# Second-table rows of the expert stage requested at the step that uses them, not three steps earlier

## The reference

```
e = top experts of the token, (512 tokens, 8 heads, 16)      # indices into both tables
a = gelu(einsum('nhkd,nd->nhk', u_tab[e], x))                # first table: 128 rows of 1024 floats per token
out = einsum('nhk,nhkd->nd', softmax(score) * a, v_tab[e])   # second table: 128 rows of 1024 floats per token
```

## Time and profile before

| | us |
|---|---|
| median of 3 runs | 3035.53 |
| lowest and highest run | 3022.3, 3048.35 |
| the profiled execution, its own time | 3030.12 |
| its span from first to last instruction | 3028.4 |
| first dot product of the expert stage starts at | 878.9 |
| last dot product, last addition of a v row start at | 2795.4, 2847.7 |

### The profile page before, as it was taken

How to read it: one execution, slowest core, us unless ns; L and a number is a source line. 1 busy time by engine, 2 the same in 40 slices (tenths; PEclk the granted TensorE clock), 3 DMA queues, 4 the chain that set the end, 5 groups by cost and what they waited for, 6 DMA issues and landing times. The chain is left out here.

```text
span 3028.4 us, 26320 instructions
## 1 busy us (share of the span) xinstructions
PE 1817.3 (60%) x7725; PEld 1085.1 (36%) x7725; DVE 1847.8 (61%) x4141; ACT 392.8 (13%) x991; POOL 1312.7 (43%) x1187
## 2 busy tenths in 40 slices
PE   3999789699805569445652565675212420685585
PEld 2356466454402124222211444572112320565311
DVE  3145367731177966678997667678546884786313
ACT  1010146420101000011100111110000100110000
POOL 1000000000036754557877545565477776775202
PEclk7999879899957879767985787658655555555597
DMA  2222220034248999999999999788578996999673
GB/s 55 90 79 89 86 84 2 1 112 152 104 147 291 346 401 353 328 358 330 341 353 364 375 354 359 292 330 302 170 264 276 338 349 234 355 327 373 235 266 112
DMA packets 279873, 740.18 MB, mean 244 GB/s; under 512 B 47921, under 2 KB 91466, under 8 KB 279154
## 3 DMA queue, kind: packets, MB, share of 16 engines
q0 software_dynamic: 156672, 564.61, 51.2%
q1 hardware_dynamic: 121890, 169.67, 16.1%
q10 hardware_dynamic: 1168, 4.23, 0.4%
HBM read 729.91 MB, written 12.56 MB: 245 GB/s over the span
## 5 line engine op out<-in xcount | busy, mean ns | idle before, releaser
L3050 POOL DMA_INDIRECT branch_rows_t<-in_v_tab,e_idx x437 | 513.1, 1174 | 328.9 <-DVE heads_t L3086 190.4
L3041 POOL DMA_INDIRECT ex_u<-in_u_tab,e_idx x257 | 287.1, 1117 | 534.8 <-POOLq L2944 431.6
L3086 DVE SCALAR_TENSOR_TENSOR heads_t<-branch_rows_t,ex_coef,heads_t 128x1024 f32<-128x1024 f32 x339 | 434.5, 1282 | 4.1 <-DMA branch_rows_t<-in_v_tab,e_idx 1.4
L3070 DVE CUSTOM_DVE_ANT_0 ex_u<-ex_u,heads_t 128x1024 f32<-128x1024 f32 x257 | 314.0, 1223 | 178.7 <-DMA ex_u<-in_u_tab,e_idx 172.5
L3070 DVE CUSTOM_DVE_ANT_0 heads_t<-heads_t 128x1024 f32<-128x1024 f32 x255 | 311.5, 1222 | 176.4 <-DMA heads_t<-in_u_tab,e_idx 167.3
L3041 POOL DMA_INDIRECT heads_t<-in_u_tab,e_idx x255 | 286.2, 1122 | 98.7 <-issue 75.5
L3143 PE MATMUL ex_y_ps<-branch_rows_t,heads_t 128*128 128x512 f32 x392 | 206.8, 664 | 117.5 <-ACT heads_t L3113 48.0
L1281 PE MATMUL cs_pp<-cs_ch,xn_t 128*128 128x256 f32 x512 | 143.4, 449 | 173.9 <-DMA cs_ch<-in_cache_cmp_kv 173.9
L788 PE MATMUL in_acc<-in_w,xn_t 128*128 128x512 f32 (+7 forms) x560 | 203.0, 519 | 8.7 <-DMA in_w<-in_w_in 8.2
L1281 PEld LDWEIGHTS cs_pp<-cs_ch,xn_t 128*128 128x128 f32 x512 | 116.2, 230 | 203.3 <-DMA cs_ch<-in_cache_cmp_kv 123.4
L3143 PEld LDWEIGHTS ex_y_ps<-branch_rows_t,heads_t 128*128 128x128 f32 x392 | 76.0, 209 | 241.5 <-issue 144.3
(11 more groups left out here) (718 smaller groups left out, 3197.4 us busy)
## 6 DMA issues: line engine op xcount, KB each, us to landing
cs_ch<-in_cache_cmp_kv SPq DMA_DIRECT2D x256, 128.0 KB, 7.3
fq_mg_wg<-in_w_gate SPq DMA_DIRECT2D x6, 2048.0 KB, 20.3
fs_mg_wg<-in_w_gate SPq DMA_DIRECT2D x6, 2048.0 KB, 9.6
in_w<-in_w_in SPq DMA_DIRECT2D x4, 2048.0 KB, 7.8
branch_rows_t<-in_v_tab,e_idx POOLq DMA_INDIRECT x437, 6.3
first_w<-in_w_gate SPq DMA_DIRECT2D x3, 2048.0 KB, 7.8
fp_wb<-in_w_branch SPq DMA_DIRECT2D x6, 1024.0 KB, 10.1
fp_wg<-in_w_gate SPq DMA_DIRECT2D x3, 2048.0 KB, 7.9
```

What stands on the lines that cost most here:

```text
L3041: pool.indirect_dma_start(out=u(s), out_offset=None, in_=i["u_tab"], in_offset=bass.IndirectOffsetOnAxis(ap=idx[:, t, m:m + 1], axis=0)).t ...
L3050: pool.indirect_dma_start(out=v(n), out_offset=None, in_=i["v_tab"], in_offset=bass.IndirectOffsetOnAxis(ap=idx[:, t, m:m + 1], axis=0)).t ...
L3070: dve.tensor_tensor_reduce(out=u(s), in0=u(s), in1=x(t), scale=1.0, scalar=0.0, op0=ALU.mult, op1=ALU.add, accum_out=dots[:, t, m:m + 1]). ...
L3086: dve.scalar_tensor_tensor(out=y(t), in0=v(n), scalar=coef[:, t, m:m + 1], in1=y(t), op0=ALU.mult, op1=ALU.add).then_inc(acc_done, 1)
```

## The change

GpSimd issues v(s - 24) at step s in place of v(s - 21), at the very step at which VectorE or TensorE uses it. The diagonals of ScalarE keep their 21.

```
@@ mix_prompt, the gpsimd program
-                    n = s - LAG + AHEAD
+                    n = s - LAG
                     if 0 <= n < NS:
                         t, m = at(n)
                         if n == V_MOVES:
                             pool.wait_ge(beside.ended, merged)
                         if n >= NV_BUF:
                             mixed(pool, n - NV_BUF)
                         pool.indirect_dma_start(out=v(n), ...)
```

## The result

The changed kernel takes 3049.3 us (median of 14 executions, 3040.61 to 3055.65), the kernel before 3035.32 us (14 executions, 3022.3 to 3048.35) on the same chip: ratio 1.0045, 95% interval 1.0029 to 1.0061. The forecast was 3027 us, 0.3% less; it is 0.45% more. The profiled execution has a span of 3048.3 us, against 3028.4.

What follows compares the result with a forecast made beforehand. Gather DMA, VectorE and GpSimd were taken to stand within 15% of one another, so it was read window by window. The terms, -9 - 3 - 2 + 4 + 1 = -9 us, took the 3035.5 us median to 3027 us; range 2996 to 3068 us.

Steps and rivals of the forecast that it cites:

- part 1: 1050 to 1400 and 1650 to 1900 us, GpSimd with slack: u's lead brings half of 17.5 unfilled us, -9 us.
- part 2: Windows with GpSimd full: lead can't be used; -3 us for late windows, between 0 and -15; side gathers' stretches 0.
- contention: Slower rival: TensorE's 16 waits for the compression's loads grow by two gathers each, +46 us, 3080 us; chance 0.04.
- Part 1's second window: 1650 to 1900 us: DMA share 1.01, nothing unfilled; VectorE waits longer for TensorE (55.6 us), so nothing counted.
- Part 3: At 2149 us: GpSimd's 12.87 us wait for TensorE before a v row goes, but only two u rows come earlier, -2 us.
- Part 4: v without a reserve: additions wait for v in part of the steps; bounds nothing and 45 us, taken +4 us.
- Part 5: The ends: start unaffected; at the tail 24 v rows left after the last u row, not 21; +1 us.
- the faster rival: Same as "The lead is worth its waits": 2962 us at its end, 2990 us if half comes; chance 0.15.
- v just in time: Slower rival: additions wait 0.4 us in each of the full windows' 113 steps, nothing gives it back, 3075 us; chance 0.08.
- The lead is worth its waits: Faster rival: all 66 us of u waits in two windows and 12 of the late ones go, 2962 us; chance 0.15.

Runs made afterwards that it cites:

- e9: Against the kernel before (v 21 slots behind): 24 behind in steps 0 to 199 and from 460 on; 3085.14 us, ratio 0.9962.
- e11: Against the kernel before (v 21 slots behind): 24 behind only from step 460 on; 3084.68 us, ratio 0.9957.
- e12: Against the kernel before (v 21 slots behind): 24 behind in steps 224 to 343 and from 460 on; 3030.93 us, ratio 0.9989.
- e14: Against the kernel before (v 21 slots behind): 24 behind only from step 460 on, same as e11 on another chip; 3022.08 us, ratio 0.9961.
- e1: Against the kernel before (v 21 slots behind): 24 behind only in steps 200 to 223, the compression's weights; 3045.96 us, ratio 1.0029.
- e2: Against the changed kernel (v 24 slots behind): 21 behind in steps 200 to 223; 3046.02 us, ratio to the kernel before 1.0040.
- e4: Against the changed kernel (v 24 slots behind): 21 behind in steps 200 to 223 and 344 to 459; 3028.91 us, ratio to the kernel before 0.9984.
- e7: Against the kernel before (v 21 slots behind): 24 behind only in steps 344 to 459, the side gathers' stretches; 3123.11 us, ratio 1.0035.
- e8: Not the layer: GpSimd issues five times 24 gathers, beside VectorE idle, dot products, additions, and both with pauses, compared with one another; 240.26 us.

## Why the prediction was wrong

The sum ended at -9 us; the changed kernel is 14 us slower. Three steps failed: that half of the unfilled DMA share could be had (part 1), that the side gathers' stretches keep their length because the count for a step is the same (part 2), and that contention costs nothing because "what the loads lose the gathers have already got". The time still lies inside 2996 to 3068 us, and that is luck: losses of 26 us and a gain of 12 us, none of them in the sum at near its size, cancel in part. The terms, by their own numbers:

- *Part 1, -9 us: measured 0.* The wait for u did go, nearly all of it (49.1 to 3.8 us in the first window). The step that failed is the one from the DMA share: that half of the 17.5 unfilled us could be had. Where the waits for u went, the waits for the side lane took over 44 of the 45 us. e9 equals e11, and steps 0 to 210 are 701.6 to 711.1 us with 21 behind and 702.1 to 711.7 with 24.
- *Part 1's second window, counted within it as nothing: measured +9 us* (e12 less e14), and up to +9 us for the weights just ahead of it (e1: 0.0029 of 3032). I had put the contention rival at "what the loads lose the gathers have already got". For the six loads of the weights it matters when GpSimd pauses (4.6 against 20.8 us, and 4.7 with the wait put back). For the compression the times say that the old pause is worth 9 us; VectorE's wait for TensorE there grew by 24 us (55.6 to 79.7), and through which load, no run tells.
- *Part 2, -3 us, "the lead can't be used": wrong on both sides.* The side gathers' stretches, put at 0, cost 13 us in the steps of the changed kernel and 17 in the times of e2 and e4 (7 to 11 by e7 on its chip). At the end, where I had GpSimd at 94%, the lead was worth 12 us (e14 0.9961 of 3034), the one gain of the change. The fullness was read from busy time at the durations of before. A busy time that holds 1.04 us issues isn't a fixed length: 0.94 us when VectorE is idle, up to 3.01 us when not.
- *Part 3, -2 us.* The wait of 12.87 us went, and as the text had it the same stage waited for VectorE instead. The timeline after, answering to the earlier trace rows, shows the new wait in full (14.91 us where 12.87 and 0.64 had been, so nothing came back):

```profile
2166.61 0.94 POOL L3050 DMA_INDIRECT branch_rows_t<-in_v_tab,e_idx  x1 [0.30 <-issue]
2182.46 1.91 POOL L2064 DMA_INDIRECT sk_t<-tmp_cand,sk_cand_at  x1 [14.91 <-DVEq L175]
```

- *Part 4, +4 us: the right place, mis-sized.* The waits of VectorE for v are 65.7 us, not 5 to 40, and those for u fell by 148 us, not 10 to 40. In the full steps the sum of the two didn't change (81.5 and 80.2 us in e2 and e4); what grew there was the issues, a price that the sum didn't hold.
- *Part 5, +1 us:* not resolved.

Of the signs, these came as written: GpSimd's wait before line 3050 fell to near nothing and moved in part to line 3041, and the DMA shares stayed above 0.95 (0.96 and 0.99). One sum of the text is off: by its own terms the faster rival at half of its 66 + 12 us gives 3035 - 39 + 5 = 3001 us, not 2990. And its range ends at 3068 us, below the 3075 us of the rival most of which it was to hold.

Of the rivals, "v just in time" is nearest: its place (the full windows) and its sign are right, its price of 45 us is about three times the 13 to 17 us measured, and its mechanism is only half of it: the additions do wait, but the loss is in the issues. "Contention" was right for the weights and the compression, at some 9 us and not 46; TensorE's waits for the loads, on which it was priced, went from 173.9 us in 16 times only to 178.2 us in 13. "The lead is worth its waits" holds at the end only, with 12 us.

Do the parts add up? End -12, compression +9, side gathers +17: +14 us, of which e2, which has just these, shows 12. The 17 us are themselves e2 less e4, so the test of the sum is e4, with end and compression alone: -3 us by the parts, and 0.9984 or -5 us (-3 by the medians) measured. The weights alone are +9 us (e1), but on top of the rest only 1.5 (the changed kernel less e2, 1.0045 less 1.0040): in the steps the weights cost 17 us more than in e2 (98.6 against 81.4), and the compression behind them 12 us less (475.9 against 487.5). Why it does, no run tells.

## What to carry over

An issuing engine that waits isn't only losing time: a pause of it can be when loads of another queue get through, so before a wait is taken away or moved, look which loads start inside it. A distance between two streams needn't be one constant: read each stretch for which engine is full, and set it stretch by stretch, as here (24 behind is worth 12 us at the end, and costs 26 us ahead of it). And waits that vanish from one line are a gain only where the next thing on that engine wasn't waiting too: compare the waits of all its lines over the same window.

## What the runs showed of the hardware

- An indirect DMA's issue on GpSimd takes 0.94 us beside an idle VectorE. When it starts during a 128x1024 float32 dot product or addition (1.22 and 1.3 us), with more than some 0.13 us of that left, it ends 0.8 us after it: up to 1.98 us in all in e8, and 3.01 us where the addition followed the dot product at once (kernel before, 2452.68 us).
- Six loads issued by SyncE took 4.6 us after a pause of GpSimd's gathers and 20.8 us behind a run of them; the page loads behind them took 1.09 us each beside gathers without a pause. That GpSimd's own waits can be what another queue lives on was not in any of my sums.
